# Feed-forward products of one decoder layer by Strassen's scheme, with the intermediate rows in DRAM

## What is computed

```
x += W_o( sig(g_a) * W_oa(DilatedSWA(h)) + sig(g_b) * W_ob(RGLRU(h)) ),  h = RMSNorm(x)
x += W_down(relu(W_up(RMSNorm(x)))^2)          # up: 1024 -> 4096, down: 4096 -> 1024
x += sigmoid(W_pg(RMSNorm(x))) * W_pe(p)
```

## Time and profile before

| | us |
|---|---|
| median of 3 runs (2204.84 to 2206.73) | 2206.58 |
| the profiled execution, its own time | 2204.05 |
| its span, first to last instruction | 2202.1 |
| PE busy | 2170.7 (99%) |
| DVE / ACT / POOL busy | 727.8 / 662.6 / 528.5 (33% / 30% / 24%) |
| DMA, mean over the span | 74 GB/s |

### The profile page before, as it was taken

The page is one execution under the profiler, slowest core; times in us unless marked ns, Lnnn a source line. Parts: engine busy times, 40 slices in busy tenths (PEclk is TensorE's granted clock), DMA queues, the critical chain, the costliest instruction groups (busy, mean ns, idle before and its releaser), DMA issues.

```text
span 2202.1 us, 31813 instructions
## 1 busy us (share of the span) xinstructions
PE 2170.7 (99%) x13686; PEld 2125.1 (97%) x13686; DVE 727.8 (33%) x1243; ACT 662.6 (30%) x1092; POOL 528.5 (24%) x233
## 2 busy tenths in 40 slices
...
GB/s 276 55 84 110 97 82 120 100 83 112 106 85 110 117 47 68 44 44 45 40 49 49 60 97 49 48 49 49 39 51 46 42 45 51 46 44 43 49 137 79
DMA packets 56894, 161.99 MB, mean 74 GB/s; under 512 B 8859, under 2 KB 21255, under 8 KB 55699
## 3 DMA queue, kind: packets, MB, share of 16 engines
...
...
## 4 chain that ended last, share of the span: by engine, by line
PE 94%; DVE 2%; ACT 1%; issue 1%; DMA 1%; POOL 1%; SPq 0%; ACTq 0%; DVEq 0%
PE ps L1404 60%; PE ps L1049 22%; PE pair L1139 2%; PE ps L1057 2%; PE pair L1099 2%; PE ps L1083 2%; PE pair L1123 1%; PE ps L1114 1%; PE ps L1435 0%; PE ps L1066 0%; PE pair L1425 0%; POOL w_lo L1653 0%; DMA wp_raw<-w_pin 0%; PE ps L441 0%; DMA pe_dram<-pe_stage 0%
## 5 line engine op out<-in xcount | busy, mean ns | idle before, releaser
L1653 POOL TENSOR_TENSOR w_lo<-w_raw,w_hi 128x1024 fp32r<-128x1024 f32 (+1 forms) x119 | 289.0, 2429 | 588.8 <-ACT w_hi L1471 588.8
L1049 PE MATMUL ps<-act_lo,w_hi 128*128 128x352 f32 x1056 | 352.5, 334 | 3.1 <-DVE qkt L858 1.8
L1049 PE MATMUL ps<-act_hi,w_lo 128*128 128x352 f32 x1056 | 340.6, 323 | 0.0
L1049 PE MATMUL ps<-act_hi,w_hi 128*128 128x352 f32 x1056 | 339.7, 322 | 0.0
L1404 PE MATMUL ps<-act_lo,w_hi 128*128 128x352 f32 x1536 | 332.4, 324 | 3.2 <-POOL w_lo L1653 3.2
L1404 PE MATMUL ps<-act_hi,w_lo 128*128 128x352 f32 x1536 | 331.1, 323 | 0.0
L1404 PE MATMUL ps<-act_hi,w_hi 128*128 128x352 f32 x1536 | 330.6, 323 | 0.0
L706 POOL TENSOR_TENSOR w_lo<-w_raw,w_hi 128x1024 fp32r<-128x1024 f32 (+1 forms) x44 | 106.2, 2413 | 666.8 <-ACT w_hi L718 666.8
L1404 PEld LDWEIGHTS ps<-act_lo,w_hi 128*128 128x128 f32 x1536 | 261.6, 189 | 3.8 <-POOL w_lo L1653 3.8
L1404 PEld LDWEIGHTS ps<-act_hi,w_lo 128*128 128x128 f32 x1536 | 263.8, 188 | 0.0
L1404 PEld LDWEIGHTS ps<-act_hi,w_hi 128*128 128x128 f32 x1536 | 260.8, 188 | 0.0
...
## 6 DMA issues: line engine op xcount, KB each, us to landing
w_raw<-w_qkv SPq DMA_DIRECT2D x36, 512.0 KB, 4.5
w_raw<-w_up SPq DMA_DIRECT2D x32, 512.0 KB, 3.6
w_raw<-w_down SPq DMA_DIRECT2D x32, 512.0 KB, 3.6
kcache<-kc SPq DMA_DIRECT2D x16, 512.0 KB, 3.9
...
e_bc<-lse_dram SPq DMA_DIRECT2D x12, 528.0 KB, 5.4
x_res<-x_t SPq DMA_DIRECT2D x8, 528.0 KB, 11.1
pe_dram<-pe_stage SPq DMA_DIRECT2D x8, 528.0 KB, 4.6
```

The costliest lines, as they stand in the source:

```text
L1049: ins = pe.matmul(pj[c][:, 0:CH], w[:, b % 2, k], x[:, k, c * CH:(c + 1) * CH], start=k == 0 and x is act_lo, stop=k == KD - 1 and w is w_lo)
L1653: pool.tensor_tensor(w_lo[:, s, 0:nk], w_raw[:, s, 0:nk], w_hi[:, s, 0:nk].bitcast(F32), ALU.subtract).then_inc(S["wlo"], 1)
```

## The change

The feed-forward block is written as 2x2 block products, and each of them in seven products of half size in place of eight (Strassen's scheme in Winograd's form). Halves: of the rows (TH = 528 each), of the contraction (even and odd k-tiles) and of two neighbouring output tiles.

- 48 units replace the 64 products. Units 0 to 15 (`r < NPAIR`) make two `up` tiles each: 7 products of 4 k-tiles. Units 16 to 47 are `down`: 8 blocks (NBLK) of four hidden tiles, in each 4 units (NDP), each for two output tiles: 7 products of 2 k-tiles. A product streams 2 x 264 columns per weight tile and part: 24 matmuls in an `up` unit's product, 12 in a `down` unit's. The order is 2, 6, 7, 5, (1 of the next unit), 3, 4.
- The Winograd sums are partly made in PSUM: products 1, 6, 5, 3 follow each other in one pair of banks without clearing, 7 and 4 in another, 2 in a third; between them the running sum is read out: in `up` units by ACT (after 1, 6, 7, 3; `copy_chain`) and by DVE (after 2, 5, 4; `add_chain`), in `down` units all seven by DVE, added to X (`add_residual`). 6, 5, 3 and 4 each wait for the read-out of the one before in their banks.
- Weights: a unit's raw weights are 1 MB (`up`) or 512 KB (`down`), loaded in two halves; four sums of them are made by DVE (`weight_sums`, `last_weight_sum`; 512 or 256 columns each), and the seven operands are split by ACT (`piece_hi`) and POOL (`piece_lo`), 4 products ahead in `up`, 8 in `down`.
- The seven right-hand operands of `up` (op0 to op6) are made once around `wo` 7 and unit 0, in the places of act_hi/act_lo/b_hi/b_lo. X is stored to `x2_dram` at `wo` and loaded again (`reload_x`) before the `down` units need it, because X's place serves as two of the three stages of hidden rows.
- Hidden rows: relu (DVE), square (ACT), four Winograd sums (`hidden_sums`, DVE), then all seven operands of a unit are stored to `hid_dram` (7 x 528 columns, 1.8 MB, `store_hidden`) and come back per block in seven loads of 528 KB (`load_hidden`) through four buffers (`hraw`), to be split by ACT (`hidden_hi`) and DVE (`hidden_lo`), one block ahead of the PE. `hidden_after` says after which product each is split.
- Around it: the column sums of the norm are 4 matmuls of 264 columns after unit 0's product 7 (`column_quarters`), and the Ln of `inverse_rms` must be through before unit 1's product 1 may write those banks. `load_unit(1)` waits for the sum of squares, since it shares its place. The loads of `pe_out` are issued when the last product is through. The gate's own work is the same, in other places.

```diff
+OPERAND = {1: 0, 2: 1, 3: 2, 5: 3, 6: 4, 7: 5, 4: 6}
+HORDER = ((0, 1), (1, 2), (4, 6), (5, 7), (3, 5), (2, 3), (6, 4))
+STAGES = (0, 1, 2, 0, 1, 2, 0, 1, 2, 0, 1, 2, 0, 2, 1, 2)
...
     out = [("wo", m) for m in range(KD)]
-    mlp = [(n, KD * b + y) for b in range(FB) for n in ("up", "down") for y in range(KD)]
-    return first + lru + merge + out + mlp + [("gt", m) for m in range(KD)]
...
+        self.order = [(0, 1)]
+        for r in range(NU):
+            self.order += [(r, 2), (r, 6), (r, 7), (r, 5)] + ([(r + 1, 1)] if r + 1 < NU else []) + [(r, 3), (r, 4)]
+        self.at = {p: n for n, p in enumerate(self.order)}
...
+    def hidden_after(self, n):
+        r, m = self.order[n]
+        if r == NPAIR - 1:
+            return [(0, j) for j, (_, k) in enumerate(HORDER) if k == m]
+        first = self.at[NPAIR, 2]
+        if n < first:
+            return []
+        b, y = divmod(n - first, 7 * NDP)
+        return [(b + 1, y // 4)] if y % 4 == 0 and b + 1 < NBLK else []
...
+        def load_unit(r):
+            y = r % 2
+            src = a["w_us"][r] if r < NPAIR else a["w_ds"][r - NPAIR]
...
+            elif r == 1:
+                sp.wait_ge(S["ssq"], KD)
+            else:
+                sp.wait_ge(S["wlo_p"], U.done(r - 2, 4))
+            sp.dma_start(raw(r)[:, 0:2], src[:, 0:2]).then_inc(S[f"raw{y}a"], 16)
+            if r == 1:
+                sp.wait_ge(S["tot"], 1)
+            sp.dma_start(raw(r)[:, 2:4], src[:, 2:4]).then_inc(S[f"raw{y}b"], 16)
+        def store_hidden(r):
+            name, before_it = stored(r)
+            sp.wait_ge(*since("tsum", 4 * (r + 1)))
+            sp.dma_start(hid_dram[r // 2][:, :, r % 2], staged(r)[:, 1:8]).then_inc(S[name], 16)
+        def load_hidden(n, j):
+            c = 7 * n + j
...
+            if c == 0:
+                name, before_it = stored(12)
+                sp.wait_ge(*since(name, before_it + 16))
+            if c > 3:
+                sp.wait_ge(*since("hid_lo", c - 3))
+            sp.dma_start(k2(hraw[:, c % 4]), hid_dram[n][:, HORDER[j][0]]).then_inc(S[f"hraw{c % 4}"], 16)
+        def reload_x(r, tiles_of):
+            name, before_it = stored(r)
+            sp.wait_ge(*since(name, before_it + 16))
+            for m in tiles_of:
+                sp.wait_ge(*since(f"x2_{m % 2}", 16 * (KD // 2)))
+                sp.dma_start(X[:, m], x2_dram[m]).then_inc(S[f"tile{m}_loaded"], 16)
+        def feed():
+            store_x2(KD - 1)
+            load_unit(1)
+            for r in range(NPAIR):
+                if r:
+                    store_hidden(r - 1)
+                if r == NPAIR - 1:
+                    reload_x(NPAIR - 2, range(KD // 2))
+                load_unit(r + 2)
+                if r == NPAIR - 2:
+                    for j in range(4):
+                        load_hidden(0, j)
+            for j in range(4, 7):
+                load_hidden(0, j)
+            for r in range(NPAIR, NU):
+                n, dp = divmod(r - NPAIR, NDP)
+                if r == NPAIR:
+                    store_hidden(r - 1)
+                    reload_x(NPAIR - 1, range(KD // 2, KD))
+                if r + 2 < NU:
+                    load_unit(r + 2)
+                if n + 1 < NBLK:
+                    for j in range(2 * dp, min(2 * dp + 2, 7)):
+                        load_hidden(n + 1, j)
...
+            pe.wait_ge(S["wlo_p"], n + 1)
...
+            elif (r, m) == (1, 1):
+                pe.wait_ge(S["ln"], 2)
+            elif (r, m) == (1, 2):
+                pe.wait_ge(S["ln"], 2)
+            before_m = {6: 1, 5: 6, 3: 5, 4: 7}.get(m)
+            if before_m:
+                pe.wait_ge(*since(f"e{before_m}", r + 1))
+            elif m == 1 and r >= 2:
+                pe.wait_ge(*since("e3", r - 1))
+            elif m in (2, 7) and r:
+                pe.wait_ge(*since("e2" if m == 2 else "e4", r))
+            if r >= NPAIR:
+                pe.wait_ge(*since("hid_lo", 7 * U.block(r) + j + 1))
...
+                for w, x in ((whi, ol[o]), (whi, oh[o]), (wlo, oh[o])):
+                    for q in range(2):
+                        ins = pe.matmul(out[:, q], w[:, k], x[:, at + k, q * QT:(q + 1) * QT],
+                                        start=m in (1, 2, 7) and k == 0 and x is ol[o], stop=k == nk - 1 and w is wlo,
+                                        skip_group_check=True)
+            ins.then_inc(S["strip"], 1)
...
+        def piece_hi(n):
+            r, m = U.order[n]
+            src, hi, lo = piece(n)
+            if n < 4:
+                act.wait_ge(S["mm"], done("wo", KD - 2 + n // 2))
+            else:
+                act.wait_ge(S["strip"], U.free[n])
+            if m in (1, 2, 4):
+                act.wait_ge(*since(f"raw{r % 2}{'b' if m == 4 else 'a'}", 16 * (r // 2 + 1)))
+            else:
+                act.wait_ge(*since("wsum", 4 * r + {5: 1, 6: 2, 7: 3, 3: 4}[m]))
+            act.activation(hi, src, ACT.Copy).then_inc(S["whi_p"], 1)
+        def copy_chain(r, m):
+            act.wait_ge(S["strip"], U.done(r, m))
+            if m == 1:
+                name, before_it = stored(r)
+                if before_it:
+                    act.wait_ge(*since(name, before_it))
+                if r in (1, 2):
+                    act.wait_ge(S["op_lo"], 20 + 4 * r)
...
+        def hidden_hi(n, j):
+            c = 7 * n + j
+            act.wait_ge(*since(f"hraw{c % 4}", 16 * (c // 4 + 1)))
+            act.wait_ge(S["strip"], U.done(NPAIR - 1 if n < 2 else NPAIR + NDP * (n - 1) - 1, HORDER[j][1]))
+            act.activation(operand(n, j)[0], k2(hraw[:, c % 4]), ACT.Copy).then_inc(S["hid_hi"], 1)
...
+            for n, (r, m) in enumerate(U.order):
+                if r < NPAIR and m in (1, 6, 7, 3):
+                    copy_chain(r, m)
+                if n == 0:
+                    operand_hi(5, last)
+                    operand_hi(4, last)
+                if (r, m) == (NPAIR, 2):
+                    square_hidden(r - 1)
+                for x in U.pieces_after.get(n, ()):
+                    piece_hi(x)
+                if n == 0:
+                    squared(KD - 1)
+                elif n == 1:
+                    for k in range(4):
+                        operand_hi(3, k)
+                elif n == 2:
+                    for k in range(4):
+                        operand_hi(2, k)
+                        operand_hi(6, k)
+                elif n == 3:
+                    inverse_rms()
+                if m == 2 and 1 <= r < NPAIR:
+                    square_hidden(r - 1)
+                for b, j in U.hidden_after(n):
+                    hidden_hi(b, j)
...
+        def weight_sums(r):
+            A, W = raw(r), sums(r)
+            for h in "ab":
...
+            else:
+                dve.wait_ge(S["wlo_p"], U.done(r - 1, 5))
+                dve.wait_ge(*since("wsum", 4 * r))
+            dve.tensor_tensor(W[:, 0], A[:, 2], A[:, 3], ALU.add).then_inc(S["wsum"], 1)
+            dve.wait_ge(*since("wsum", 4 * r + 1))
+            dve.tensor_tensor(W[:, 1], W[:, 0], A[:, 0], ALU.subtract).then_inc(S["wsum"], 1)
+            dve.tensor_tensor(A[:, 2], A[:, 0], A[:, 2], ALU.subtract).then_inc(S["wsum"], 1)
...
+        def add_chain(r, m):
+            at, prior = {2: (1, 1), 5: (3, 7), 4: (2, 6)}[m]
+            dst = c2(staged(r)[:, at])
+            dve.wait_ge(*since(f"e{prior}", r + 1))
+            dve.wait_ge(S["strip"], U.done(r, m))
+            dve.tensor_tensor(dst, dst, chain(r, m), ALU.add).then_inc(S[f"e{m}"], 1)
+        def add_residual(r, m):
+            prior, now = {1: (2, 0), 2: (1, 1), 3: (3, 0), 4: (6, 1), 5: (7, 1), 6: (4, 0), 7: (5, 0)}[m]
+            if now:
+                dve.wait_ge(*since(f"e{prior}", r + 1))
+            elif r >= NPAIR + NDP:
+                dve.wait_ge(*since(f"e{prior}", r - NDP + 1))
+            else:
+                dve.wait_ge(S[f"tile{2 * (r - NPAIR) + (m in (6, 7))}_loaded"], 32)
+            dst = c2(residual(r, m))
+            dve.wait_ge(S["strip"], U.done(r, m))
+            dve.tensor_tensor(dst, dst, chain(r, m), ALU.add).then_inc(S[f"e{m}"], 1)
+        def relu_hidden(r):
+            h = staged(r)
+            dve.wait_ge(S["rstd"], 1)
+            dve.wait_ge(*since("e2", r + 1))
+            dve.scalar_tensor_tensor(out=h[:, 1], in0=h[:, 1], scalar=0.0, in1=G[3][:, 0:TH], op0=ALU.max, op1=ALU.mult).then_inc(S["relu"], 1)
+            dve.wait_ge(*since("e3", r + 1))
+            dve.scalar_tensor_tensor(out=h[:, 0], in0=h[:, 0], scalar=0.0, in1=G[3][:, TH:T], op0=ALU.max, op1=ALU.mult).then_inc(S["relu"], 1)
+            dve.wait_ge(*since("e4", r + 1))
+            dve.wait_ge(*since("e5", r + 1))
...
+        def hidden_sums(r):
+            h = staged(r)
+            dve.wait_ge(*since("sq_h", 2 * r + 1))
+            dve.tensor_tensor(h[:, 4], h[:, 0], h[:, 1], ALU.subtract).then_inc(S["tsum"], 1)
+            dve.wait_ge(*since("sq_h", 2 * r + 2))
```

(44 more changed lines are left out.)

473 lines of the change are left out of this document (356 added, 117 removed), and 3 rows, old and new, of the table again.

## The result

The changed kernel takes 2295.58 us (median; 2293.50 to 2300.78) against 2206.65 before: 1.0408 times the time, 95% interval 1.0390 to 1.0426. The forecast was 2214, range 2176 to 2252. Slower was right; 82 us are missing from it.

The account below looks back on a forecast made before the run. PE, busy 99% of the span, was taken as the bound. Matmuls -77, start +7, between up and down +39.5, down blocks +38.5 and tail +0.8 gave +8.8 on 2204.05: 2213, forecast as a median of 2214, range 2176 to 2252.

Parts of the forecast that it names:

- Matmuls, -77: Feed-forward products on PE: 5376 matmuls of 264 columns at 123.3 ns, 662.9 us against 740.0 before.
- Rivals 2 and 4: 264-column matmuls: 2, at the 112 ns weight-load floor, 2153, chance 0.05; 4, at 130 ns or more, 2250, chance 0.08.
- Up, 0: Up units, 20.7 us of PE each: no added wait per unit, bounds 0 and 2; tight place product 3.
- rival 3: Up and down: DVE and POOL taking turns become the bound, slower, 2254; chance 0.20.
- Start, +7: Units 0 and 1: waits of 4.7 and 5.9, norm's matmuls and slow clock, 14.5 against 7.9 before.
- Between up and down, +39.5: Turn at units 15 to 17: PE waits for read-outs behind hidden loads, 36.7, plus 2.8 for low-clock restarts.
- In the blocks of down, +38: Down blocks: hidden operands land late, 29.5, plus 3 for POOL and 6 for clock; bounds 5 and 90.
- The clock, 6 of the 38: Down: PE at half clock behind gaps of 3.4, 1.3 us lost each, six gaps, four of five so.
- Tail, +0.8: End of the kernel: one read-out before the gate's first product, 0.8 us.
- rival 1: Down blocks and boundary: loads land in time, waits shrink, faster, 2175; chance 0.22.

Follow-up runs that it names:

- e3: Against the changed kernel, SyncE's loads between up and down reordered: hidden operands ahead of the reload of X and of the store of unit 15's hidden rows; 2280.89 us.
- e1: Against the changed kernel, in the blocks of down the two loads of hidden operands issued ahead of the unit's weights; 2211.67 us.
- e2: Against the changed kernel, the next block's hidden operands loaded one unit earlier, those of unit 16 left in place; 2212.25 us.
- e9: Against the changed kernel, loads unchanged, ACT's and DVE's split of each hidden operand in down two products later in their order; 2225.13 us.
- e6: Against the changed kernel, three edits at once: e2's order, e3's order, and up's weight sums later in DVE's order; 2192.25 us.
- e7: Against e6, between up and down: two hidden loads ahead of a store, unit 18's weights ahead of X's reload, DVE read-outs ahead of split and sums; 2185.36 us.
- e8: Against e7, in the last block the gate's rows made one at a time, the second later, on ACT, POOL and DVE; 2181.72 us.
- e10: Against e8, unit 17's weights loaded ahead of the store of rows 14 and X's reload, unit 18's ahead of the store of rows 15; 2174.39 us.

## Why the prediction was wrong

- **Matmuls, -77:** -86. 121.7 ns, where the line through the rows gave 121.5 and I took 123.3: 9 us too dear. Rivals 2 and 4 are out. With 121.5 the sum of the prediction would have been -1, no change, so that it said slower hung on this term; what made the kernel slower is the step in down below.
- **Up, 0:** 12.2. The place was named, with the condition: the read-out of 5 after 14.8. Its turns were counted as two to three; they are five, of 1.1 us: rival 3's condition for up, at less than half of its price.
- **Start, +7:** right; gaps and slow are 13.9, said 14.5. The first distance of 6.8 holds the norm's sums, 1.9 where 0.9 was said (the four matmuls of the program show as eight records), and then an idle time of 4.8, said 4.7; the second gap is 3.4, said 5.9. That the total fits is in part luck.

```profile
1366.60 1.94 PE L1647 MATMUL ps<-tmp,ones 128*128 128x264 f32 x8
1373.33 0.78 PE L1682 MATMUL ps<-op_lo,up_hi 128*128 128x264 f32 x2 [4.78 <-ACT hid_stage L1875]
```

- **Between up and down, +39.5:** 44.5, of which 37.6 gaps against 36.7. The places are right (27.5 before (16,5), said 28), but e3 shows that the hidden load alone holds half of it, and DVE's own queue the other half; the 7.3 before (16,6) came as 4.2, with 3.9 and 2.1 before products 3 and 5 of unit 15. The slow clock behind them was 6.9, said 2.8.
- **In the blocks of down, +38: this step failed.** It measured 106.5. Mechanism, places and releaser were right, and e1, e2 and e9 show them; the sizes were not. The landing was taken at 4.7 after the unit's start; in blocks 1 to 6 ACT begins on the operands at 5.2 to 7.3, 6.35 in the mean, and in block 3 on the first at 5.95. Counted from the load's own issue that is 5.0, where 2.3 and the bytes at 416 GB/s gave 3.9; the page's median over all 56 such loads is 5.9. In the window from 1912.5 to 1914.5 the core's DMA moved 244 GB/s, from 1915.5 to 1917.5 370.

```profile
1912.50:1914.50 2.00, 2.00 (x19) 2.00 (x18) 1.94 (x4) 0.47 (x2) 1.16 (x2) 1.00 0.71 244
1915.50:1917.50 2.00, 0.96 (x8) 0.75 (x7) 0.00 (x0) 0.00 (x0) 0.00 (x0) 1.00 0.95 370
```

  The third operand of that block (ACT, next row) landed 6.6 after its unit's start of 1928.43.

```profile
1935.04 1.09 ACT L1887 ACTIVATE op_hi<-hid_raw 128x1056 fp32r<-128x1056 f32 x1 [3.08 <-DMA hid_raw<-hid_dram]
```

  A wait is landing less slack, and the slack was right (1.3, 3.5 and 4.2 to 4.5 measured; 1.3, 3.7 and 4.4 by the prediction's own numbers). In block 3, 1.2 of landing made 3.4 into 4.7, and 1.9 made 1.0 into 3.1; a block's three gaps are 10.4 together in the mean, said 4.7. Summed over blocks 0 to 6 that is 67.3 of gaps where 29.5 were said, and 3 more for waits on POOL. Why the landings are longer is open; two loads share the queue behind the weights. Block 7, priced at 0, is 11.1: I had left out the gate's rows, which take turns with POOL's sums of squares.
- **The clock, 6 of the 38:** 28. I had taken one slow stretch of 1.3 a block, in four blocks of five. There are two in each of blocks 1 to 6, behind the first and the second gap, three in block 7 and one in block 0, 1.2 to 2.6 each; behind the third gap of blocks 1 to 6 there is one slow start, 0.1.
- **Tail, +0.8:** 1.6; and 4.2 ahead of the stretch, for which I had nothing.
- Of the rivals, 3 named 2254 and a DVE that is full. DVE isn't: e1 does the same work in 42.5 a block. For rival 1, loads in time are not enough: e1 and e2 are still 0.2 to 0.3% slower than the kernel before. With the turn and up mended as well, in e6, e7, e8 and e10, the scheme is 0.7 to 1.4% faster.
